# Output-projection weights loaded early, and 42 of the 80 output-projection products placed between the closing steps of the fourth head pair

## The reference, cut to what matters

```python
cols = (rmsnorm(x, norm_mix_g) @ w_in).astype(f32)
ml_out, C1, n1, m1, conv1 = mlstm_mixer(cols[..., :ML_COLS], ...)      # 4 heads of 128 columns
rw_out, S1, shift1 = rwkv7_mixer(cols[..., ML_COLS:], shift0, ...)     # 8 heads of 64 columns
mix = jnp.concatenate([ml_out, rw_out], axis=-1)                       # 1024 columns
x = x + mix @ w_out                                                    # the output projection
x = x + peer(rmsnorm(x, norm_ffn_g), peer_w_q, peer_sub_keys, peer_u, peer_v)
```

```python
S1, ys = lax.scan(step, S0, (r, decay, k, v, kk, a))
y = head_norm(jnp.swapaxes(ys, 0, 1), gn_g, GN_EPS) + gn_b
y = y + (jnp.sum(r * k * r_k, axis=-1, keepdims=True) * v).reshape(B, T, W)
return y * g, S1, cols[:, -1]
```

## Time and profile before

| | |
|---|---|
| median of 3 runs | 2716.7 us (2709.44 to 2717.69) |
| the profiled execution's own time | 2715.1 us |
| its span in the trace | 2713.0 us |
| TensorE busy | 2400.8 us, 88% of the span |
| VectorE busy | 1698.9 us, 63% |
| ScalarE busy | 786.1 us, 29% |
| mean granted TensorE clock | 0.915 of full speed |

### The profile page before, as it was taken

The page is one execution under the profiler, slowest core; times in us unless marked ns, Lnnn a source line. Parts: engine busy times, 40 slices in busy tenths (PEclk is TensorE's granted clock), DMA queues, the critical chain, the costliest instruction groups (busy, mean ns, idle before and its releaser), DMA issues.

```text
span 2713.0 us, 35239 instructions
## 1 busy us (share of the span) xinstructions
PE 2400.8 (88%) x13799; PEld 1861.6 (69%) x13799; DVE 1698.9 (63%) x2934; ACT 786.1 (29%) x932; POOL 328.1 (12%) x256
## 2 busy tenths in 40 slices
PE   6999965776858996989999999999679999999996
PEld 3556635555733675868878878878558888888885
DVE  1113436456430102999999969999667777777775
ACT  2112323223200103444435425424322222222221
POOL 3000000000000001431141241141100000100010
PEclk8999976668759998999999999999889999999998
DMA  4111100000012220336636535636576666666652
GB/s 155 62 32 56 49 12 1 2 6 6 7 49 107 70 97 32 124 140 216 239 149 239 211 147 212 238 146 237 203 275 248 237 232 232 241 244 244 246 193 76
DMA packets 154541, 387.44 MB, mean 143 GB/s; under 512 B 10016, under 2 KB 83520, under 8 KB 139712
## 3 DMA queue, kind: packets, MB, share of 16 engines
q1 hardware_dynamic: 124416, 251.73, 26.6%
q0 software_dynamic: 18496, 67.15, 6.8%
q10 hardware_dynamic: 11520, 67.11, 6.3%
HBM read 309.85 MB, written 75.56 MB: 142 GB/s over the span
## 4 chain that ended last, share of the span: by engine, by line
PE 49%; DVE 17%; ACT 2%; DMA 1%; issue 1%; ACTq 0%; SPq 0%; DVEq 0%
PE bank L1430 26%; PE bank L1380 13%; PE bank L1390 3%; PE bank L1329 3%; PE bank L1351 2%; PE bank L1352 2%; DVE hot_a L1912 1%; DVE sc L1878 1%; DVE sca L1946 1%; DVE si L1877 1%; DVE si L1880 1%; DVE sca L1943 1%; PE bank L1361 1%; DVE u_lo L1885 1%; DVE hot_e L1911 1%
## 5 line engine op out<-in xcount | busy, mean ns | idle before, releaser
L1430 PE MATMUL bank<-w_hi,v_hi 128*128 128x512 f32 x1024 | 399.4, 390 | 41.2 <-DVE w_lo L2001 41.2
L1380 PE MATMUL bank<-xhi,u_hi 128*128 128x512 f32 x1024 | 412.0, 402 | 14.9 <-POOL u_lo L541 14.9
L1380 PE MATMUL bank<-xlo,u_hi 128*128 128x512 f32 x1024 | 406.2, 397 | 0.0
L1380 PE MATMUL bank<-xhi,u_lo 128*128 128x512 f32 x1024 | 405.9, 396 | 0.0
L1430 PE MATMUL bank<-w_lo,v_hi 128*128 128x512 f32 x1024 | 399.1, 390 | 0.0
L1430 PE MATMUL bank<-w_hi,v_lo 128*128 128x512 f32 x1024 | 399.1, 390 | 0.0
L2013 DVE TENSOR_TENSOR mixT<-bank,mixT 128x512 f32<-128x512 f32 x256 | 173.3, 687 | 184.6 <-PE bank L1430 184.6
L924 ACT ACTIVATE v_hi<-wring 128x4096 fp32r<-128x4096 f32 x32 | 116.3, 3636 | 494.7 <-PE bank L1430 470.7
L1430 PEld LDWEIGHTS bank<-w_hi,v_hi 128*128 128x128 f32 x1024 | 192.8, 188 | 81.3 <-issue 41.3
L1380 PEld LDWEIGHTS bank<-xhi,u_hi 128*128 128x128 f32 x1024 | 194.7, 190 | 58.0 <-issue 15.3
L971 PE MATMUL bank<-xnT,wbuf 128*128 128x512 f32 x416 | 230.6, 637 | 0.0
(11 more groups left out here) (484 smaller groups left out, 3646.9 us busy)
## 6 DMA issues: line engine op xcount, KB each, us to landing
u_raw<-in_pu SPq DMA_DIRECT2D x64, 1024.0 KB, 4.8
wring<-in_pv SPq DMA_DIRECT2D x32, 2048.0 KB, 16.2
act_scratch<-actb ACTq DMA_DIRECT2D x64, 512.0 KB, 3.5
gate_scratch<-gst ACTq DMA_DIRECT2D x16, 2048.0 KB, 7.1
wts<-act_scratch SPq DMA_DIRECT2D x32, 1024.0 KB, 5.1
gring<-gate_scratch SPq DMA_DIRECT2D x32, 1024.0 KB, 10.9
wbuf<-in_w_in SPq DMA_DIRECT2D x4, 2048.0 KB, 10.2
wring<-in_w_q SPq DMA_DIRECT2D x4, 2048.0 KB, 7.7
```

Of the source, the lines that this page charges most:

```text
L1380: ins = mm(bank[b][:, :], lhsT, rhs[:, 0:SEQ], **on)
L1430: ins = mm(bank[c][:, :], lhsT, rhs[:, q, e, :], **on)
```

## The change

It has five parts.

1. A buffer `w_o` of 2 x 8 x 512 values a partition takes the memory from `u_hi` on (the shifted columns `ext_r` during the mixers). `xg`, the gate's input, which lay in this part of the memory and is read until the end of `post(3)`, moves to another place.
2. SP loads both halves of `w_out` into `w_o` after `chan_ready` 4, that is after `prep(3)`, ahead of the stores of pair 2.
3. `x1` now lies in the memory of the score buffer `sca`. SP loads x after the chunk work of pair 3, ahead of the stores of pair 3. ACT waits for the stores of `x1` before it writes scores.
4. TensorE draws products from a list of 42, results 0 to 5 times slices 0 to 6, after each step of `post(3)`: two after each of the first eight steps, four after the others. Before the first it waits for the weights, for `mix_ready` 7, `y0_ready` 12 and `bonus_ready` 4. After `mix_ready` 8 come the 38 others. The results use banks 0 to 5 in turn, since `post` uses 6 and 7.
5. After `mix_ready` 8 SP loads the gain, two panels of `w_q` and the sub-keys; xs is copied and `x1` stored before the third and fourth panel. The semaphore counts follow.

```diff
@@ SBUF @@
+        xg = sb("xg", [128, NT], scope=mixers)
...
-        x1_sc = ExitStack()
-        x1 = sb("x1", [128, 5, D], scope=x1_sc)
-        x1_sc.close()
+        w_out_sc = ExitStack()
+        w_o = sb("w_o", [128, 2, KD, 512], scope=w_out_sc)
+        w_out_sc.close()
...
+        x1 = sca[:, :, :].rearrange("p t n -> p (t n)")[:, 0:5 * D].rearrange("p (t d) -> p t d", t=5)
@@ SP @@
             for p in range(4):
+                if p == 2:
+                    sp.wait_ge(S("chan_ready"), 4)
+                    for half in range(2):
+                        sp.dma_start(w_o[:, half, :, :], w_out.rearrange("(k p) n -> p k n", p=128)[:, :, 512 * half:512 * half + 512]
+                                     ).then_inc(s_ring[half], 16)
+                if p == 3:
+                    sp.wait_ge(S("gh_copied"), 12)
+                    sp.wait_ge(S("y0_ready"), 12)
+                    for t, (t0, n) in enumerate(TILES):
+                        sp.dma_start(x1[0:n, t, :], x_d[t0:t0 + n, :]).then_inc(s_x1, 16)
                 sp.wait_ge(S("rstate_ready"), p + 1)
...
@@ ACT @@
+            act.wait_ge(s_x1s, 16 * 5)
             for pos, t in enumerate(ORDER):
...
@@ PE @@
-            for _ in post(3):
-                pass
-
+            def out_product(jj, kt):
+                half, t = divmod(jj, 5)
+                t0, n = TILES[t]
+                return mm(bank[jj % 6][0:n, :], mixT[:, kt, t0:t0 + n], w_o[:, half, kt, :], start=kt == 0, stop=kt == KD - 1)
+
+            todo = iter([(jj, kt) for jj in range(6) for kt in range(KD - 1)])
+            for i, _ in enumerate(post(3)):
+                if i == 0:
+                    for half in range(2):
+                        pe.wait_ge(s_ring[half], 16)
+                    pe.wait_ge(S("mix_ready"), 7)
+                    pe.wait_ge(S("y0_ready"), c_gh)
+                    pe.wait_ge(S("bonus_ready"), 4)
+                for _ in range(2 if i < 8 else 4):
+                    for jj, kt in [next(todo, (-1, -1))]:
+                        if jj >= 0:
+                            out_product(jj, kt)
+            for jj, kt in todo:
+                out_product(jj, kt)
             pe.wait_ge(S("mix_ready"), 8)
-            for half in range(2):
-                pe.wait_ge(s_ring[half], 16)
-                for t, (t0, n) in enumerate(TILES):
-                    jj = 5 * half + t
-                    if jj >= 4:
-                        pe.wait_ge(S("x1_ready"), jj - 3)
-                    for kt in range(KD):
-                        ins = mm(bank[jj % 4][0:n, :], mixT[:, kt, t0:t0 + n], wring[:, half, kt, :], start=kt == 0,
-                                 stop=kt == KD - 1)
-                    ins.then_inc(S("outproj_done"), 1)
+            for jj in range(10):
+                if jj >= 6:
+                    pe.wait_ge(S("x1_ready"), jj - 5)
+                for kt in range(KD - 1 if jj < 6 else 0, KD):
+                    ins = out_product(jj, kt)
+                ins.then_inc(S("outproj_done"), 1)
```

More of the change, by code:

```diff
@@ L159, in hybrid_step @@
         xwa = sb("xwa", [128, NT], scope=rwk)
-        xg = sb("xg", [128, NT], scope=rwk)
         X = {n: sb("rw_" + n, [128, NT], scope=rwk) for n in
@@ L209, in hybrid_step @@
         first = ExitStack()
-        x1_sc = ExitStack()
-        x1 = sb("x1", [128, 5, D], scope=x1_sc)
-        x1_sc.close()
+        w_out_sc = ExitStack()
+        w_o = sb("w_o", [128, 2, KD, 512], scope=w_out_sc)
+        w_out_sc.close()
         u_hi = sb("u_hi", [128, 2, KD, GU * 128], f32r, scope=first)
-        pad = sb("pad", [128, D], scope=first)
         xhi = sb("xhi", [128, KD, SEQ], f32r, scope=first)
@@ L384, in _, with load_w_q @@
             sp.wait_ge(s_out, 16 * 19)
-            for t, (t0, n) in enumerate(TILES):
-                sp.dma_start(x1[0:n, t, :], x_d[t0:t0 + n, :]).then_inc(s_x1, 16)
-            sp.dma_start(gain[:, :], gffn_d.partition_broadcast(128)).then_inc(s_x1, 16)
-            sp.dma_start(subT[:, :, :], sub_d).then_inc(s_sub, 16)
[L390 to L398, removed]
-                    for half in range(2):
-                        sp.dma_start(xs[64 * half:64 * half + 64, :], xf[0:SAMP, 0, :]).then_inc(s_xs, 16)
+            sp.dma_start(gain[:, :], gffn_d.partition_broadcast(128)).then_inc(s_sub, 16)
+            def load_w_q(c):
+                sp.dma_start(wring[:, c % 2, :, :], w_q.rearrange("(k p) n -> p k n", p=128)[:, :, 512 * c:512 * c + 512]
+                             ).then_inc(s_ring[c % 2], 16)
+            load_w_q(0)
+            load_w_q(1)
+            sp.dma_start(subT[:, :, :], sub_d).then_inc(s_sub, 16)
+            sp.wait_ge(S("xf_ready"), 5)
+            for half in range(2):
+                sp.dma_start(xs[64 * half:64 * half + 64, :], xf[0:SAMP, 0, :]).then_inc(s_xs, 16)
             sp.wait_ge(S("x1_ready"), 10)
@@ L404, in _ @@
                 sp.dma_start(x1_d[t0:t0 + n, :], x1[0:n, t, :]).then_inc(s_x1s, 16)
+            for c in (2, 3):
+                sp.wait_ge(S("qproj_done"), 4 * (c - 1))
+                load_w_q(c)
             sp.wait_ge(S("qproj_done"), 12)
@@ L884, in copy_quad @@
                     act.dma_start(chunk, gst[:, k // 8, :, :]).then_inc(s_gst[k // 8], 16)
-            act.wait_ge(s_x1s, 16 * 5)
             act.wait_ge(S("scores_done"), 5)
@@ L1317, in _ @@
                 rest()
-            for _ in post(3):
-                pass
-            pe.wait_ge(S("mix_ready"), 8)
-            for half in range(2):
-                pe.wait_ge(s_ring[half], 16)
-                for t, (t0, n) in enumerate(TILES):
-                    jj = 5 * half + t
-                    if jj >= 4:
-                        pe.wait_ge(S("x1_ready"), jj - 3)
-                    for kt in range(KD):
-                        ins = mm(bank[jj % 4][0:n, :], mixT[:, kt, t0:t0 + n], wring[:, half, kt, :], start=kt == 0,
-                                 stop=kt == KD - 1)
-                    ins.then_inc(S("outproj_done"), 1)
+            def out_product(jj, kt):
[5 more added lines that the diff above has]
+                if i == 0:
+                    for half in range(2):
+                        pe.wait_ge(s_ring[half], 16)
[8 more added lines that the diff above has]
+                out_product(jj, kt)
+            pe.wait_ge(S("mix_ready"), 8)
+            for jj in range(10):
[4 more added lines that the diff above has]
+                ins.then_inc(S("outproj_done"), 1)
             for t, (t0, n) in enumerate(TILES):
@@ L1354, in _ @@
             pe.wait_ge(S("qT_ready"), 16)
-            pe.wait_ge(s_sub, 16)
+            pe.wait_ge(s_sub, 32)
             for pos, t in enumerate(ORDER):
@@ L1853, in _ @@
             dve.wait_ge(S("mix_ready"), 8)
-            dve.wait_ge(s_x1, 16 * 6)
+            dve.wait_ge(s_x1, 16 * 5)
             for half in range(2):
@@ L1860, in _ @@
                     dve.wait_ge(S("outproj_done"), jj + 1)
-                    TT(x1[0:n, t, cs], bank[jj % 4][0:n, :], x1[0:n, t, cs], ALU.add).then_inc(S("x1_ready"), 1)
+                    TT(x1[0:n, t, cs], bank[jj % 6][0:n, :], x1[0:n, t, cs], ALU.add).then_inc(S("x1_ready"), 1)
                     own(S("x1_ready"))
+            dve.wait_ge(s_sub, 32)
             for t, (t0, n) in enumerate(TILES):
@@ L2028, in _ @@
                         sample_add(2 * g + c // 4)
-            dve.wait_ge(s_x1, 16 * 12)
+            dve.wait_ge(s_x1, 16 * 11)
             for t, (t0, n) in enumerate(TILES):
```

## The result

| | before | changed |
|---|---|---|
| median | 2713.17 us (4 runs, 2709.44 to 2717.69) | 2678.81 us (4 runs, 2677.77 to 2682.47) |
| ratio | | 0.9875, 95% interval 0.9853 to 0.9897 |
| profiled execution, span | 2715.1, 2713.0 us | 2678.0, 2675.8 us |
| mean granted TensorE clock | 0.915 | 0.925 |

The changed kernel is 34.4 us faster by the medians and 37.1 us by the two profiled executions. The forecast was 2679 us.

The account below looks back on a forecast made before the run. TensorE was taken to stand on the chain or wait on it for 117.1 us, 776.3 to 893.4. New end 776.3 + 9.7 + 71.3 = 857.3, 36.1 us less, so 2679 from 2715.1; range 2668 to 2696.

Parts of the forecast that it names:

- The load of `w_out`: Before the output projection: loading the weights early removes TensorE's 17.8 us wait for them.
- The pauses: Closing steps of the last pair: products placed ahead of waits cover all 12.5 us of TensorE idle time.
- The faster clock for the closing steps: Last pair's closing steps: without idle time the clock rises, cutting their own products from 15.56 to 9.7 us.
- The products: Output projection: 80 products at 0.865 us each plus 2.1 us for the clock's rise, 71.3 us.
- The rise of the clock: Start of the output products: running slow until the clock rises costs 2.1 us.
- upper bound: Whole time: no overlap and half a microsecond lost at each of some ten new joints, 2684 us.
- The slack at the end: Last DVE and ACT chain: TensorE's queued work, 13.5 us, outlasts its 7.3 us, with 6 us to spare.
- What follows: After the last residual add: 10.4 us of norm and transposes and all behind them move as a whole.
- The pauses stay: Closing steps: each comes late by the products ahead, so TensorE still waits; + 12.5 us, 2691.5; 12% with partial forms.
- the change does nothing but hide the load: First product: a semaphore comes only with the end of `post(3)`, so just 17.8 us is gained; 2697 us, 2%.
- the slow clock until the end of `post(3)`: Closing steps and their 42 products stay at 1.2 GHz; 6.1 us later than before, 2721 us, 4%.
- through the whole projection: Many waits keep TensorE at 1.2 GHz for all 80 products, ending at 930.3; 2752 us, 3%.

Follow-up runs that it names:

- e7: Changed kernel with early loads kept, but all 80 output products held until the last pair's mixer slice is finished; 2697.42 us.
- e2: Changed kernel with all 42 products in one block behind the first closing step instead of spread between steps; 2700.12 us.
- e9: Same program as e6, measured again; 2675.61 us, ratio 0.9855.
- e6: Changed kernel with 12 of the 42 products moved earlier, between steps of the last pair's sample chunk; 2664.08 us, ratio 0.9820.
- e4: Changed kernel with the output weights loaded only after the last pair's chunk work, just ahead of x; 2694.01 us.
- e8: As e6, with 14 products in the sample chunk, two more filling the gap before the masks; 2657.64 us, ratio 0.9786.
- e0: The changed kernel measured again, nothing altered; 2679.78 us.
- e5: Changed kernel with x loaded only after the last slice of the mixer output, as before the change; 2679.48 us.

## Why the prediction was right, point by point

- **The load of `w_out`.** Forecast 17.8 us. e7 measures 17.5, and no other wait took its place. Its early issue shows no cost: in the changed kernel `chan_ready` 4 came at 675.1 us, the halves landed at most 12.8 us after their issue, and TensorE asked for the weights at 775.6.
- **The pauses.** Forecast: 12.5 us, all covered. e2 has the early weights and the products, but not the placement, and shows 12.6 us of TensorE idle; the changed kernel shows none. Of the 18.1 us between e7 and the changed kernel (99.7 and 81.6), 12.6 are these pauses; the faster closing steps of the next point give 6.7, and the products take 1.2 back (72.6 against 71.4).
- **The faster clock for the closing steps.** Forecast: from 15.56 to 9.7 us, with up to 1.5 less for overlap. The chain shows 1.97 + 7 x 0.26 + 0.96 + 0.89 + 2 x 1.03 + 1.22 = 8.9 us. So 6.7 us, not 5.9.
- **The products.** Forecast 71.3 us; the chain gives 81.5 - 8.9 = 72.6. The rise of the clock cost less than forecast (3.00 instead of 1.73 us for the first two products, 1.3 us against 2.1), but the groups take longer than 0.865 us a product: 0.16 to 0.18 more for each group up to the state part of y (1.91 us for two products instead of 1.73), 0.03 and 0.12 for the two between the 128-wide pairs, 0.5 for the last 48 products, 2.1 in all. The sum priced the joints only in its upper bound. The two errors of this and the point before nearly cancel: 81.0 forecast, 81.5 measured.
- **The slack at the end.** Forecast 6 us and `mix_ready` 8 at about 818. The slice came at 815.6, in a stretch that began 2.65 us earlier. The ten products ahead of TensorE's wait for it began at 813.07 and ended, at 0.865 us each, at about 821.7: 6.1 us to spare. The 7.38 us of the first add are DVE's wait, which takes in one product more.
- **What follows.** Forecast to move as a whole; it lost 1.1 us. From the start of the last add to the end of the span the twelve traces took between 1819.2 (e7) and 1824.5 us (e9), and the changed kernel alone 1820.6 and 1822.6 in its two, so 1.1 us says nothing.
- **The hit itself.** That 2678.81 lies 0.2 us from 2679 is luck. The forecast took 36.1 us from 2715.1, the time of one execution; by the medians the gain is 34.4 us, from 2713.17. The two differences, 1.7 and 1.9 us, cancel. The stretch is the fair test: 36.1 us less forecast, 35.7 measured.
- **The rivals.** The pauses stay (2691.5), the change does nothing but hide the load (2697), the slow clock until the end of `post(3)` (2721) or through the whole projection (2752): none happened, since TensorE had no wait and the clock stood at 1.00 from 777.7 on. A kernel that only hides the load is e7, and took 2697.42. The slow clock was a real danger all the same: e9 shows 27 us of it, in a list that follows one product with 64-wide work. At 4% it was rated low for a pattern that I had only compared with a stretch of small products. (The prediction reads 0.50 for all of 742 to 822; in that trace the clock fell at 743.9. Nothing hangs on it.) The rule cited from the Trainium skill's page "TensorE: Matmul & The Clock Gate", section "A second HAM failure mode: psum-queue depth-cycling", is about a clock that goes down and up again where TensorE pauses briefly between groups of matmuls. In the changed kernel there were no such pauses (81.48 of 81.5 us busy), so its trace does not test the rule; in e6 and e9, with one gap of 1.7 us and not many small ones, the traces agree in part: the clock fell, once, behind it.

## What to carry to other kernels

When the last link of a chain has nothing beside it, look for work of the next stage whose inputs are complete but for one part: a sum over eight slices can be seven eighths done. Place it ahead of the waits, in groups just longer than each wait; the same work in one block gave nothing (e2), and with its weights late it gave back 12 us (e4). Then look at the stretch before, and fill the gaps within the placed work too: behind one of 1.7 us the clock fell in both traces that have it, for 7 us in one and 27 in the other (e6, e9), and with 0.39 us there it did not (e8).

## What the runs showed of the hardware

- TensorE can be busy without a pause and stay at 1.2 GHz: 24.00 of 24 us at 0.50 in e9, with single full-array products between 64-wide ones, while the same program came back to 1.00 after 7 us in e6's trace. It makes about 10 us of difference for one program (99.0 and 109.6 us for one stretch).
- How soon the clock rises after the output products begin was no fixed price. After TensorE had stood still it took 3.3 us (e7), 3.7 (before) and 5.2 (e4); in the changed kernel, e0 and e5, where it had been busy with closing products for 2 us just before, 2.1 to 2.3. The 2.1 us of lost time that the forecast took for the rise was one draw.
- The same gap of 2.6 us ahead of pair 2's variance products came with a fall of the clock in e8 and e9 and without one in e6, where the clock stood at 1.00 until 753.8.
- Products and state steps in turn cost more than the two alone: 1.91 us for two products between 64-wide steps against 1.73 in a row, 0.18 us for each such group in a queue that never idles.
